# Attention on one core: the value products in two groups a job, and three PSUM banks that all score pieces, turned shifts and row sums share

## The reference, cut to what matters

```python
def gqa_block_attention(q, k, v):
    ...
    def one_block(q_blk):
        s = jnp.einsum('bqhgd,bkhd->bhgqk', q_blk, k, preferred_element_type=F32) * scale
        pr = jax.nn.softmax(s, axis=-1).astype(v.dtype)
        return jnp.einsum('bhgqk,bkhd->bqhgd', pr, v)
```

## Time and profile before

| | us |
|---|---|
| median of 3 runs | 3422.48 (3421.16 to 3422.75) |
| profiled execution: its own time, its span | 3418.13, 3416.3 |
| TensorE matmul busy over the span | 3074.5 (90%) |
| VectorE, ScalarE, GpSimd busy | 1508.5, 739.8, 1044.1 |
| attention stage: first score matmul, last scaling | 841.28, 1380.38 |
| turned shifts of jobs 1 and 14 (L1173) | 892.32, 1315.19 |

### The profile page before, as it was taken

One profiled execution on the slowest core, in us unless ns is written; L12 is line 12 of the kernel. 1 busy time (PEld: TensorE's weight loads), 2 busy tenths in 40 slices (PEclk: granted clock), 3 DMA queues, 4 the chain that ended last, 5 costly groups with the idle time before them and its releaser, 6 DMA issues.

```text
span 3416.3 us, 28734 instructions
## 1 busy us (share of the span) xinstructions
PE 3074.5 (90%) x10264; PEld 1501.8 (44%) x10264; DVE 1508.5 (44%) x2461; ACT 739.8 (22%) x1549; POOL 1044.1 (31%) x953
## 2 busy tenths in 40 slices
PE   6996999998999999999398995886888999999995
PEld 3553554444444443444244442554434444444442
DVE  2343782345666665222333224356104444544446
ACT  1123754311333333010111112322101000000001
POOL 0001870000676677000100001227003444555444
PEclk8997999999999999999599997897999999999998
DMA  6000422002300000100678997001002111121101
GB/s 250 19 0 0 118 87 90 25 25 109 132 1 1 1 1 1 63 19 6 238 293 308 345 348 267 4 0 38 25 29 70 37 37 37 38 73 38 37 13 56
DMA packets 138109, 279.97 MB, mean 82 GB/s; under 512 B 24904, under 2 KB 80880, under 8 KB 125808
## 3 DMA queue, kind: packets, MB, share of 16 engines
q1 hardware_dynamic: 123120, 228.65, 19.0%
q10 hardware_dynamic: 10240, 32.71, 2.6%
q0 software_dynamic: 4608, 16.78, 1.3%
HBM read 231.98 MB, written 46.15 MB: 81 GB/s over the span
## 4 chain that ended last, share of the span: by engine, by line
PE 68%; issue 12%; POOL 8%; DVE 5%; DMA 4%; ACT 2%; SPq 0%; ACTq 0%; POOLq 0%; DVEq 0%
PE ps L2906 16%; PE ps L2922 6%; PE ps L1400 6%; PE ps L469 6%; PE ps L1021 5%; PE ps L1740 5%; POOL arena_b L1274 4%; PE ps L932 3%; PE ps L2711 3%; DMA ring<-in_w_up 3%; PE ps L1759 2%; PE ps L2040 2%; PE ps L876 1%; PE ps L2684 1%; PE ps L840 1%
## 5 line engine op out<-in xcount | busy, mean ns | idle before, releaser
L1274 POOL TENSOR_TENSOR arena_b<-arena_b 128x512 f32<-128x512 f32 x288 | 356.9, 1269 | 176.6 <-ACT arena_b L1256 176.5
L2878 POOL TENSOR_TENSOR arena_b<-arena_b,arena_d 128x512 f32<-128x512 f32 x132 | 165.8, 1270 | 374.4 <-DVE arena_d L3013 372.6
L1292 DVE TENSOR_REDUCE arena_b<-ps 128x1 f32<-128x512 f32 (+1 forms) x384 | 213.9, 597 | 147.9 <-PE ps L1163 147.7
L2991 DVE TENSOR_TENSOR arena_d<-arena_d,ps 128x512 f32<-128x512 f32 x154 | 101.9, 685 | 385.9 <-PE ps L2906 385.9
L1740 PE MATMUL ps<-ring,arena_a 128*128 128x512 f32 x496 | 231.0, 621 | 26.7 <-issue 16.2
L1256 ACT ACTIVATE arena_b<-ps 128x512 f32<-128x512 f32 x320 | 173.7, 595 | 335.0 <-PE ps L1198 335.0
L1163 PE MATMUL ps<-arena_d,arena_a 64*128 64x512 f32 (+1 forms) x768 | 207.1, 535 | 3.1 <-DVE arena_b L1283 2.9
L3010 DVE TENSOR_TENSOR arena_b<-arena_b,ps 128x512 f32<-128x512 f32 x264 | 174.7, 685 | 48.6 <-POOL arena_b L2878 26.0
L1192 PE MATMUL ps<-arena_a,arena_d 64*128 64x512 f32 x640 | 195.4, 618 | 0.8 <-ACT arena_b L1256 0.8
L469 PE MATMUL ps<-arena_b,ring 128*128 128x512 f32 x384 | 166.9, 592 | 0.8 <-ACT arena_b L448 0.8
L1021 PE MATMUL ps<-ring,arena_b 128*128 128x512 f32 x384 | 167.4, 592 | 0.0
(11 more groups left out here) (514 smaller groups left out, 5038.5 us busy)
## 6 DMA issues: line engine op xcount, KB each, us to landing
ring<-in_w_gate SPq DMA_DIRECT2D x42, 1024.0 KB
ring<-in_w_up SPq DMA_DIRECT2D x42, 1024.0 KB
ring<-in_w_down SPq DMA_DIRECT2D x42, 1024.0 KB
ring<-in_w_in SPq DMA_DIRECT2D x10, 2048.0 KB, 12.3
ring<-in_w_mod SPq DMA_DIRECT2D x32, 512.0 KB, 3.9
xslots<-arena_c SPq DMA_DIRECT2D x1, 15872.0 KB, 47.9
arena_a<-xslots ACTq DMA_DIRECT2D x31, 512.0 KB, 5.4
yslots<-arena_a ACTq DMA_DIRECT2D x31, 512.0 KB, 5.1
```

The source lines that it names most:

```text
L1274: eng.tensor_tensor(acc, first, prT[n % NPR], ALU.add).then_inc(s_pa, 1)
L1292: eng.tensor_reduce(mx3[j % 2][:, t, e, piece:piece + 1], ps[:, u % 3, 0:k1 - k0], AX.X, ALU.max).then_inc(s_mx, 1)
```

## The change

The value products come in two groups of five steps (`GROUP`), behind steps 4 and 9. The shifted rows take banks 3, 4 and 5 in rotation. Score pieces, turned shifts and row sums take banks 0, 1 and 2 in the order in which TensorE comes to them; a list written at build time (`takes`, `uses`, `freed`) gives each its bank and the semaphore value that frees it. The pieces are assigned to other steps, one more score piece is made ahead of the first job, and the number of `prT` buffers is 12. The turned shifts come ahead of the second value group, the row sums of the job before ahead of the first.

```diff
-        NPR = 6
+        NPR = 12
...
-        BESIDE = ((1, 2), (1, 3), (1, 5), (1, 6), (1, 7), (1, 8), (1, 10), (1, 11), (2, 0), (2, 1))
-        BEHIND = {1: (1, 4), 5: (1, 9)}
-
-        HELD = (0, 4, 6, 8)
-
-        def score_bank(n):
-            kt, e = n % 20 // 2, n % 2
-            return (3, 4)[e] if kt - 1 in HELD else 4 + e
...
+        BESIDE = ((1, 3), (1, 4), (1, 5), (1, 6), (1, 7), (1, 9), (1, 10), (1, 11), (2, 0), (2, 1))
+        BEHIND = {4: (1, 8), 9: (2, 2)}
+
+        GROUP = 5
+
+
+        uses, freed = {}, []
+
+        def takes(kind, i):
+            uses[kind, i] = len(freed)
+            freed.append({"s": (s_mx, i + 1), "t": (s_sh, i + 1), "r": (s_o, 2 * i + 1)}[kind])
+
+        def takes_pair(j, pair):
+            for e in range(2):
+                takes("s", 24 * j + 2 * pair + e)
+
+        def shared(kind, i):
+            return uses[kind, i] % 3
+
+        def wait_shared(eng, kind, i):
+            if uses[kind, i] >= 3:
+                eng.wait_ge(*freed[uses[kind, i] - 3])
...
@@ pe_att
-                    if u >= 3:
-                        eng.wait_ge(s_mx, u - 2)
-                    eng.matmul(ps[:, u % 3, 0:k1 - k0], qT[rows, pr, q0:q0 + P], kT[rows, pr // 2, k0:k1],
+                    wait_shared(eng, "s", u)
+                    eng.matmul(ps[:, shared("s", u), 0:k1 - k0], qT[rows, pr, q0:q0 + P], kT[rows, pr // 2, k0:k1],
...
             def turn_shifts(j):
                 eng.wait_ge(s_mc, 6 + 6 * (j + 1))
-                if j >= 1:
-                    eng.wait_ge(s_ex, 20 * (j - 1) + 2 * (NT - 1) + 1)
-                if j >= 2:
-                    eng.wait_ge(s_o, 2 * (j - 1))
+                wait_shared(eng, "t", j)
...
-                    bank = score_bank(n + e)
...
-                    eng.matmul(ps[:, bank, :], kT[rows, pr // 2, kt * P:(kt + 1) * P], qT[rows, pr, qs],
+                    if n + e >= 3:
+                        eng.wait_ge(s_ex, n + e - 2)
+                    eng.matmul(ps[:, 3 + (n + e) % 3, :], kT[rows, pr // 2, kt * P:(kt + 1) * P], qT[rows, pr, qs],
                                start=True, stop=False)
...
             def row_sums(j):
                 eng.wait_ge(s_pa, 18 * (j + 1))
-                if j + 1 < NJOB:
-                    eng.wait_ge(s_sh, j + 2)
-                    eng.wait_ge(s_ex, 20 * (j + 1) + 2 + 1)
-                else:
-                    eng.wait_ge(s_o, 2 * j)
-                    eng.wait_ge(s_ex, 20 * NJOB - 1)
+                wait_shared(eng, "r", j)
...
             scores(1, 0)
             turn_shifts(0)
             scores(1, 1)
+            scores(1, 2)
             for j in range(NJOB):
                 for kt in range(NT):
                     shifted(j, kt)
                     if j + BESIDE[kt][0] < NJOB:
                         scores(j + BESIDE[kt][0], BESIDE[kt][1])
-                    if kt in HELD:
-                        continue
-                    for i in range(10 * j + kt - (2 if kt - 1 in HELD else 1), 10 * j + kt):
-                        if i >= 0:
-                            pv(i // 10, i % 10)
-                    if kt == 2 and j >= 1:
+                    if kt == GROUP - 1 and j >= 1:
                         row_sums(j - 1)
                     if kt == NT - 1 and j + 1 < NJOB:
                         turn_shifts(j + 1)
+                    if kt % GROUP == GROUP - 1:
+                        for i in range(kt + 1 - GROUP, kt + 1):
+                            pv(j, i)
                     if kt in BEHIND and j + BEHIND[kt][0] < NJOB:
                         scores(j + BEHIND[kt][0], BEHIND[kt][1])
-            pv(NJOB - 1, NT - 1)
             row_sums(NJOB - 1)
...
@@ dve_att, scale
                 eng.wait_ge(s_sum, j + 1)
-                step(eng, eng.reciprocal(rec, ps[:, 3, :]), s_o, 2 * j + 1)
+                if j >= 1:
+                    eng.wait_ge(s_o, 2 * j)
+                step(eng, eng.reciprocal(rec, ps[:, shared("r", j), :]), s_o, 2 * j + 1)
...
@@ dve_att, its order
             largest(1, 1)
+            largest(1, 2)
             for j in range(NJOB):
                 for kt in range(NT):
                     if j + BESIDE[kt][0] < NJOB:
                         largest(j + BESIDE[kt][0], BESIDE[kt][1])
-                    if kt == 2 and j >= 1:
+                    if kt == GROUP - 1 and j >= 1:
                         scale(j - 1)
-                    if kt in BEHIND and j + BEHIND[kt][0] < NJOB:
-                        largest(j + BEHIND[kt][0], BEHIND[kt][1])
                     if kt == 7 and j + 1 < NJOB:
                         split(j + 1)
                     if kt == NT - 1 and j + 1 < NJOB:
                         shifts(j + 1)
+                    if kt in BEHIND and j + BEHIND[kt][0] < NJOB:
+                        largest(j + BEHIND[kt][0], BEHIND[kt][1])
```

More of the change, by code:

```diff
@@ L1119, in build @@
         NJOB = 2 * KT
-        NPR = 6
+        NPR = 12
         PIECE = ((0, HALF), (HALF, L), (L, NK))
-        BESIDE = ((1, 2), (1, 3), (1, 5), (1, 6), (1, 7), (1, 8), (1, 10), (1, 11), (2, 0), (2, 1))
-        BEHIND = {1: (1, 4), 5: (1, 9)}
-        HELD = (0, 4, 6, 8)
-        def score_bank(n):
-            kt, e = n % 20 // 2, n % 2
-            return (3, 4)[e] if kt - 1 in HELD else 4 + e
-        prT = [view(arena_b, i * HALF, HALF) for i in range(NPR)]
+        BESIDE = ((1, 3), (1, 4), (1, 5), (1, 6), (1, 7), (1, 9), (1, 10), (1, 11), (2, 0), (2, 1))
[13 more added lines that the diff above has]
+                eng.wait_ge(*freed[uses[kind, i] - 3])
+        prT = ([view(arena_b, i * HALF, HALF) for i in range(6)] + [view(arena_t, i * HALF, HALF) for i in range(4)]
+               + [view(arena_b, 6912 + i * HALF, HALF) for i in range(2)])
         prs = [[view(arena_b, 3072 + (2 * i + e) * HALF, HALF) for e in range(2)] for i in range(2)]
@@ L1147, in build, with turned_shifts @@
         s_sum, s_o = sem("row_sums"), sem("output_scaled")
+        for pair in range(12):
+            takes_pair(0, pair)
+        takes_pair(1, 0)
+        takes("t", 0)
+        takes_pair(1, 1)
+        takes_pair(1, 2)
+        for j in range(NJOB):
+            for kt in range(NT):
+                if j + BESIDE[kt][0] < NJOB:
+                    takes_pair(j + BESIDE[kt][0], BESIDE[kt][1])
+                if kt == GROUP - 1 and j >= 1:
+                    takes("r", j - 1)
+                if kt == NT - 1 and j + 1 < NJOB:
+                    takes("t", j + 1)
+                if kt in BEHIND and j + BEHIND[kt][0] < NJOB:
+                    takes_pair(j + BEHIND[kt][0], BEHIND[kt][1])
+        takes("r", NJOB - 1)
+        def turned_shifts(j):
+            return ps[:, shared("t", j), 0:256].bitcast(BF16)
         def pe_att(eng):
@@ L1167, in turn_shifts @@
                 eng.wait_ge(s_mc, 6 + 6 * (j + 1))
-                if j >= 1:
-                    eng.wait_ge(s_ex, 20 * (j - 1) + 2 * (NT - 1) + 1)
-                if j >= 2:
-                    eng.wait_ge(s_o, 2 * (j - 1))
+                wait_shared(eng, "t", j)
                 for t in range(4):
-                    mm = eng.transpose(turned_b[:, t * P:(t + 1) * P],
+                    mm = eng.transpose(turned_shifts(j)[:, t * P:(t + 1) * P],
                                        mcat[j % 2][:, t, :, :].rearrange("p e c -> p (e c)"), identb)
@@ L1197, in shifted @@
                     rows = slice(HD * e, HD * e + HD)
-                    eng.matmul(ps[:, score_bank(n + e), :], oneb[rows, :], shT[j % 2][rows, :], start=False, stop=True
+                    eng.matmul(ps[:, 3 + (n + e) % 3, :], oneb[rows, :], shT[j % 2][rows, :], start=False, stop=True
                                ).then_inc(s_sst, 1)
@@ L1213, in row_sums @@
                 eng.wait_ge(s_pa, 18 * (j + 1))
-                if j + 1 < NJOB:
-                    eng.wait_ge(s_sh, j + 2)
-                    eng.wait_ge(s_ex, 20 * (j + 1) + 2 + 1)
-                else:
-                    eng.wait_ge(s_o, 2 * j)
-                    eng.wait_ge(s_ex, 20 * NJOB - 1)
+                wait_shared(eng, "r", j)
                 for e in range(2):
-                    mm = eng.matmul(ps[HD * e:HD * e + HD, 3, :], ones[:, 0:HD], prs[j % 2][e], start=True, stop=True)
+                    mm = eng.matmul(ps[HD * e:HD * e + HD, shared("r", j), :], ones[:, 0:HD], prs[j % 2][e], start=True, stop=True)
                 mm.then_inc(s_sum, 1)
@@ L1255, in act_att @@
                     eng.wait_ge(s_pa, 18 * j + 2 * (max(kt, 1) - 1) + e + 1)
-                eng.activation(prT[n % NPR], ps[:, score_bank(n), :], ACT.Exp).then_inc(s_ex, 1)
+                eng.activation(prT[n % NPR], ps[:, 3 + n % 3, :], ACT.Exp).then_inc(s_ex, 1)
         def pool_att(eng):
@@ L1291, in largest @@
                     eng.wait_ge(s_S, u + 1)
-                    eng.tensor_reduce(mx3[j % 2][:, t, e, piece:piece + 1], ps[:, u % 3, 0:k1 - k0], AX.X, ALU.max
```

(3 more changed lines are left out.)

1 line of the change is left out of this document (removed).

## The result

The changed kernel is slower: median 3499.53 us (3495.84 to 3499.63, 4 runs) against 3422.55; ratio 1.0223, 95% interval 1.0208 to 1.0237, or +77 us. (The median of 3422.55 has one run more than the 3422.48 of the table.) Predicted were 3487, in 3426 to 3516.

A forecast was written before the change was run, and what follows sets the result against it. TensorE, busy throughout steady jobs, was taken as the bound. A job became 30.83 + 3.95 stop + 2.1 clock = 36.9 us, +4.35; over the stage +64.3, so 3422.48 + 64.3 = 3487 us, range 3426 to 3516.

The forecast's parts named there:

- The operations pass at 6.9, 8.1, 9.4, 10.6 and 11.8: VectorE's five small operations splitting the maxima behind piece 11: one gets through at each end of a GpSimd add.
- Head 1 of (2, 1) at 12.85: TensorE's score product waiting for the reduction of (2, 0) head 0; its own time was 8.38, so 4.47 late.
- the 0.16 and 0.15 behind the split: After VectorE's five operations: 0.16 before the reduction of (2, 0) head 0 starts, 0.15 for the semaphore to TensorE.
- 34.78: Steady job in us without clock loss: unstalled period 30.83 plus 3.95 for TensorE's wait at (2, 1) head 1.
- The clock: Lowered TensorE clock after its stop of some 3.5 us in every job: 2.1 us lost, bounds 0 and 2.8.
- The intervals of the sum: Attention stage from turn to turn: steady jobs +56.6, first job -0.1, job 14 +3.3, last +4.5; total 64.3.
- the 0.9 for the stop ahead of the row sums: Last job: clock loss for TensorE's stop ahead of the row sums, half of one such loss.
- The 0.68 behind the row sums: TensorE's wait per job at the step behind the row sums, where reductions queue behind the 3.36 us reciprocal; predicted gone.
- six visits became two: TensorE's switches from 64-row to 64-column halves and back, 0.34 us each: four fewer a job, 1.36 saved.
- The rival of an unheld split: VectorE's small operations find GpSimd idle: 30.83 a job, -27 us, 3395; chance 0.14.
- That the clock stays up: TensorE's stop in each job loses no clock: 34.78 a job, +31.9 us, 3454; chance 0.16.
- five waits from two: How many VectorE split operations wait for GpSimd adds: five gives 34.78 a job; two gives 32.43, 3419, chance 0.06.

The follow-up runs named there:

- the stop filled: Changed kernel plus three full-width products, result overwritten, ahead of the waiting score product of piece (2, 1) head 1: 3455.70 us, ratio 1.0099.
- once the split is covered: Changed kernel with the maxima split behind the reductions of piece (2, 1) and shifts turned behind the second value group and its following score piece: 3403.49 us, ratio 0.9947.
- the kernel with narrow adds: Changed kernel with GpSimd adding only 64 of 512 columns of each exponential, so row sums are wrong: 3396.90 us, ratio 0.9924.
- one of 4.82: Stop in the changed kernel with only VectorE's maxima split moved, behind the reductions of piece (2, 1): 3499.03 us, ratio 1.0227.
- one of 0.61: Stop in the changed kernel with the last two of the maxima split's five operations left out: 3417.60 us, ratio 0.9994.

## Why the prediction was right

By its own steps, with t = 0 at step 5 (1029.97 in the trace after):

- The adds start at 1.95 and run to 14.3: measured 1.94 and 14.19. Piece 11 at 4.94: 4.93. The cast issued at 6.57: 6.57.
- The operations pass at 6.9, 8.1, 9.4, 10.6 and 11.8: they end at 6.92, 8.12, 9.36, 10.57 and 11.80.
- Head 1 of (2, 1) at 12.85: measured 12.43. The step that was off is the 0.16 and 0.15 behind the split. The 0.16 idle time in the earlier trace rows was a wait for TensorE's score product, which had just been made there; with the scores long ready the reduction starts ahead of the recorded end of the cast, and TensorE starts 0.04 behind the reduction. So a job without the clock is 34.4 to 34.5, not 34.78 (34.50 with the stop filled).
- The clock is where the sum was off. I took 2.1, within 0 and 2.8. It costs 3.0 in a steady job, beyond the upper bound: 6.4 us at 0.50 lie behind a stop of 3.05, all of it on TensorE's path. Nor is the price one number. Worked out from the mean clocks, the low stretch around the three stops of the other stage was 3.5, 6.8 and 3.3 us long, and 0.6 and 1.4 of the first two lay inside the stops (clock 0.91 and 0.81 there), where nothing runs. Here it is 6.8 in a steady job (behind the stops that end at 1042.40 and 1079.96), with 0.4 inside the stop. In the first job it was 3.4, behind a stop of 3.06 as well, and lost only 1.7:

```profile
893.67 1.12 PE L1197 MATMUL ps<-arena_d,arena_a 64*128 64x512 f32 x2 [3.06 <-DVE arena_b L1309]
...
901.19 0.70 PE L1197 MATMUL ps<-arena_d,arena_a 64*128 64x256 f32 x4
```

From the end of the stop to the second of these lines it took 7.52, in a steady job 8.88, with the stop filled 5.83. Why the same stop gives a short or a long stretch is not shown; the mean of three stops could not tell which would come here.

- The intervals of the sum: 13 steady jobs +64.7 (worked out +56.6), first job 32.39 (32.4), job 14 34.95 (35.0), last 40.11 (38.0). Together the stage is 74.4 longer, not 64.3; the stages not touched add 2.6 between the medians. These two are the 12.5 us between 3487 and 3499.5.
- Part of the fit is luck. With the stop filled the stage is 33.3 longer than before, and less the 1.5 of clock that its last interval still has (below) that is the +31.9 of the sum without the clock; but errors cancel in it. The steady jobs are 0.28 shorter than 34.78, -3.6 in all. The first job takes 32.40 even with its stop filled and the clock up, so it held none of the 2.1 that I had put there, and it is 2.1 shorter than a steady one, not the 4.5 I took. In the last interval the steps come every 1.8 us (1427.52, 1429.34, 1431.16), not every 1.35, which is some 1.4 more; the 0.9 for the stop ahead of the row sums was not lost there, where the products take 1.08 as elsewhere, but some 1.5 behind the last turn was (6.4 us from there to the next shifted row, for 4.9).
- So the term that was mis-sized is the clock, by 0.9 in a steady job and by some 10 in the stage. The mechanism (which product waits, for what, and how long) is as predicted.
- The 0.68 behind the row sums is gone, no wait stands there, and six visits became two, as said. These gains are real: 31.04 a job once the split is covered.

The rival of an unheld split (3395) is the kernel with narrow adds (3396.9; its stage is 24.2 shorter in the profile, 27 were worked out). That the clock stays up (3454) is the kernel with the stop filled (3455.7). Neither was this kernel, and their prices held within 3 us, the second by the cancelling errors above.

What told five waits from two was the rule of the Trainium skill (SBUF — State Buffer, Who interferes with whom) that casts and operations with two SBUF inputs can contend with GpSimd and that `tensor_reduce` does not. The runs agree: 1.17, 1.20, 1.17 and 1.20 beside adds of 1.23 (the first cast, issued shortly before an add's end, 0.35), 0.17 to 0.19 beside adds of 0.32; and the reduction ahead of them (L1318), from SBUF to SBUF, took 0.177 to 0.179 in all 16 jobs, in the steady ones while an add ran (1036.32, inside the run of adds from 1031.91).

What stays open: the profiles of the changed kernel and its edits spend 2036 to 2042 us behind the stage, where the one of before spends 2036. I did not test whether that is theirs or the run's.

## What to carry to other kernels

When work is bunched on the busiest engine, look for what the work between the bunches had been covering on other queues; here 1.87 us of value products stood ahead of the step that needed the bank, and GpSimd had pauses; without them the chain of five small operations grew from 2.93 to 5.23 us. Casts and two-input operations of 128x8 beside a GpSimd that never paused took one GpSimd add each here, so count their chain in GpSimd instructions, and put it where TensorE has long work that does not depend on it. And price a stop of TensorE with the slow clock behind it: here the clock cost 3.0 a job, more than the 1.7 that the change gained.

## What the runs showed that I had not expected

A stop of 3.05 us cost 3.0 us more in low clock, the like one of the first job 1.7, one of 4.82 1.8, and one of 0.61 nothing. Filling the stop with work whose result is thrown away made the kernel 44 us faster than leaving it empty.
